# Moving the low half of one weight chunk behind each of five norms from VectorE to GpSimd

## What is computed

```python
x = x + 0.5 * rmsnorm(swiglu(rmsnorm(x, pre0), ffn_in0, ffn_out0), post0)
h = rmsnorm(x, pre1)                      # the next norm needs the whole new x
x = x + rmsnorm(mixer(h), post1)
x = x + 0.5 * rmsnorm(swiglu(rmsnorm(x, pre2), ffn_in1, ffn_out1), post2)
# between layer 0 and 1: kv = rmsnorm(x, kvin) @ w_dkv, shared keys and values
```

## Time and profile before

| what | value |
|---|---|
| runs | 1562.04 us median of 3 (1561.0 to 2078.39) |
| profiled execution | 1565.18 us, span 1563.5 us |
| TensorE busy | 1488.2 us (95%) |
| VectorE busy | 910.7 us (58%) |
| ScalarE busy | 748.3 us (48%) |
| GpSimd busy | 164.9 us (11%) |
| mean granted TensorE clock | 0.979 |
| chain that ended last | TensorE 84%, VectorE 10%, ScalarE 3%, issue 2%, DMA 1% |

### The profile page before, as it was taken

One profiled execution on the slowest core, in us unless ns is written; L12 is line 12 of the kernel. 1 busy time (PEld: TensorE's weight loads), 2 busy tenths in 40 slices (PEclk: granted clock), 3 DMA queues, 4 the chain that ended last, 5 costly groups with the idle time before them and its releaser, 6 DMA issues.

```text
span 1563.5 us, 29706 instructions
## 1 busy us (share of the span) xinstructions
PE 1488.2 (95%) x11112; PEld 1388.6 (89%) x11112; DVE 910.7 (58%) x1499; ACT 748.3 (48%) x1195; POOL 164.9 (11%) x239
## 2 busy tenths in 40 slices
PE   7999998999898999999979999998999999999997
PEld 7999997999676889999969999996866678999997
DVE  4655437979765586554385555337645546655524
ACT  4555425778533455553264555334334444655422
POOL 0111000000312001110001111001023400111100
PEclk9999999999899999999999999999989999999999
DMA  5444342433321234444423434344257732544341
GB/s 202 162 145 150 140 156 90 164 131 135 117 90 57 88 108 161 144 151 139 157 108 145 151 144 158 137 153 161 71 150 229 228 135 90 179 143 159 136 155 67
DMA packets 45011, 218.43 MB, mean 140 GB/s; under 512 B 6065, under 2 KB 18482, under 8 KB 22402
## 3 DMA queue, kind: packets, MB, share of 16 engines
q1 hardware_dynamic: 38738, 192.70, 34.9%
q0 software_dynamic: 6192, 24.64, 4.8%
HBM read 210.55 MB, written 6.77 MB: 139 GB/s over the span
## 4 chain that ended last, share of the span: by engine, by line
PE 84%; DVE 10%; ACT 3%; issue 2%; DMA 1%; DVEq 0%; POOL 0%; SPq 0%; ACTq 0%
PE psum L240 15%; PE psum L241 15%; PE psum L245 14%; PE psum L292 7%; PE psum L294 7%; PE psum L293 7%; PE psum L2037 2%; PE psum L2076 2%; DVE w_lo L228 1%; ACT w_hi L221 1%; DVE x L359 1%; DVE y L355 1%; DVE h_lo L401 1%; PE psum L2063 1%; PE psum L1913 1%
## 5 line engine op out<-in xcount | busy, mean ns | idle before, releaser
L228 DVE TENSOR_TENSOR w_lo<-raw,w_hi 128x2048 fp32r<-128x2048 f32 x166 | 384.9, 2318 | 319.1 <-ACT w_hi L221 318.9
L221 ACT ACTIVATE w_hi<-raw 128x2048 fp32r<-128x2048 f32 x161 | 308.6, 1916 | 367.1 <-PE psum L294 221.9
L240 PE MATMUL psum<-h_hi,w_hi 128*128 128x320 f32 x1552 | 462.8, 312 | 6.7 <-issue 4.7
L241 PE MATMUL psum<-h_lo,w_hi 128*128 128x320 f32 x1552 | 460.4, 309 | 0.0
L240 PEld LDWEIGHTS psum<-h_hi,w_hi 128*128 128x128 f32 x1552 | 293.4, 189 | 8.5 <-issue 5.4
L241 PEld LDWEIGHTS psum<-h_lo,w_hi 128*128 128x128 f32 x1552 | 293.4, 189 | 0.5
L245 PE MATMUL psum<-h_hi,w_lo 128*128 128x320 f32 x1552 | 259.8, 309 | 0.0
L245 PEld LDWEIGHTS psum<-h_hi,w_lo 128*128 128x128 f32 x1552 | 236.0, 188 | 0.4 <-DVE w_lo L228 0.2
L292 PE MATMUL psum<-hid_hi,w_hi 128*128 (+1 forms) x704 | 217.6, 309 | 4.1 <-DVE f_g L535 4.1
L294 PE MATMUL psum<-hid_hi,w_lo 128*128 (+1 forms) x704 | 217.3, 309 | 0.0
L293 PE MATMUL psum<-hid_lo,w_hi 128*128 (+1 forms) x704 | 217.3, 309 | 0.0
(11 more groups left out here) (380 smaller groups left out, 1967.9 us busy)
## 6 DMA issues: line engine op xcount, KB each, us to landing
raw<-wts SPq DMA_DIRECT2D x166, 1024.0 KB, 4.8
h_plain<-cache_t POOLq DMA_DIRECT2D x44, 160.0 KB, 3.4
h_plain<-cache_t SPq DMA_DIRECT2D x44, 160.0 KB, 3.2
arena<-s POOLq DMA_DIRECT2D x4, 1024.0 KB, 6.5
sgs<-arena POOLq DMA_DIRECT2D x4, 1024.0 KB, 4.1
marena<-cache_t POOLq DMA_DIRECT2D x20, 160.0 KB, 3.3
marena<-cache_t SPq DMA_DIRECT2D x20, 160.0 KB, 3.0
raw<-cache_c SPq DMA_DIRECT2D x16, 128.0 KB, 3.2
```

Source lines behind the costliest of these rows:

```text
L221: act.activation(w_hi[c0 % 2][:, :], raw[c0 % 2][:, :], ACT.Copy).then_inc(hi_ready, 1)
L228: eng.tensor_tensor(w_lo[c0 % 2][:, :], raw[c0 % 2][:, :], w_hi[c0 % 2][:, :].bitcast(F32), ALU.subtract).then_inc(lo_ready, 1)
L240: pe.matmul(outs[n], wtile(w_hi, c0, n * K + k), src_hi(k), start=(k == 0), stop=False)
L241: pe.matmul(outs[n], wtile(w_hi, c0, n * K + k), src_lo(k), start=False, stop=False)
```

## The change

residual_dve loses its last step and the argument for it. GpSimd gets five calls of split_lo, for the same five chunks, each ahead of the work that stood next in its queue. split_lo is the same function: it waits for `w_hi` of the chunk and for `w_lo` of the chunk before, makes one 128x2048 subtraction, and raises lo_ready. At the first boundary the call stands ahead of the issue of the `hist` transfer.

```diff
-        def residual_dve(dve, s, pre=None, q=0, c1=None):
+        def residual_dve(dve, s, pre=None, q=0):
...
             low(KT - 1)
             square_sum(KT - 1)
-            if c1 is not None:
-                split_lo(dve, c1)
...
             ffn_pool(pool, 0)
+            split_lo(pool, BASE["gates"] + 1)
             pool.wait_ge(chunk_done, BASE["gates"])
             pool.dma_start(arena[:, A_HIST:A_HIST + 24 * DEC_B * 3], io["hist"]).then_inc(s0_landed, 16)
             gdn_in_pool(pool)
             for g in range(NG):
                 core_pool(pool, g)
+            split_lo(pool, BASE["ffn1"] + 1)
             ffn_pool(pool, 1)
+            split_lo(pool, BASE["kv"] + 1)
             kv_pool(pool)
             ffn_pool(pool, 2)
+            split_lo(pool, BASE["dq"] + 1)
             pool.wait_ge(con_landed, 32)
             pool.wait_ge(chunk_done, BASE["dq"] + 2)
...
+            split_lo(pool, BASE["ffn3"] + 1)
             ffn_pool(pool, 3)
...
-            residual_dve(dve, 0, pre=(1, gpre(1)), q=1, c1=BASE["gates"] + 1)
+            residual_dve(dve, 0, pre=(1, gpre(1)), q=1)
...
```

More of the change, by code:

```diff
@@ L2489, in _ @@
             post_dve_sum(dve, 1, full(1), c1=BASE["ffn1"] + 1)
-            residual_dve(dve, 1, pre=(2, gpre(2)), q=2, c1=BASE["ffn1"] + 1)
+            residual_dve(dve, 1, pre=(2, gpre(2)), q=2)
             dve.wait_ge(rpre_ready, 3)
@@ L2496, in _ @@
             post_dve_sum(dve, 2, half(2), c1=BASE["kv"] + 1)
-            residual_dve(dve, 2, pre=(3, gkv), q=3, c1=BASE["kv"] + 1)
+            residual_dve(dve, 2, pre=(3, gkv), q=3)
             kv_dve(dve)
@@ L2500, in _ @@
             post_dve_sum(dve, 3, half(3), c1=BASE["dq"] + 1)
-            residual_dve(dve, 3, pre=(5, gpre(4)), q=4, c1=BASE["dq"] + 1)
+            residual_dve(dve, 3, pre=(5, gpre(4)), q=4)
             mla_q_dve(dve)
@@ L2506, in _ @@
             post_dve_sum(dve, 4, full(4), c1=BASE["ffn3"] + 1)
-            residual_dve(dve, 4, pre=(6, gpre(5)), q=5, c1=BASE["ffn3"] + 1)
+            residual_dve(dve, 4, pre=(6, gpre(5)), q=5)
             dve.wait_ge(rpre_ready, 6)
```

## The result

The changed kernel takes 1581.11 us in the median of 4 runs (1575.27 to 1584.87), against 1563.08 us in the median of 4 for the kernel before on the same chip: 1.0117 times as long, 95% interval 1.0075 to 1.0158. One of the four runs before took 2078.39 us and is left out of the ratio; without it their median is 1562.04 us. That is 18.0 us more by the medians and 18.2 us by the ratio; the forecast was 19.5 us more, 1581.5 us.

A forecast was written before the change was run, and what follows sets the result against it. VectorE's residual sets the pace at the five norm boundaries; elsewhere TensorE, busy 95%, does. Boundary costs net of returns, 15.0 us, plus 4.5 us of clock gave 19.5 us more, median 1581.5 us; forecast 1575 to 1587, range 1568 to 1590.

The forecast's parts named there:

- GpSimd's time: At each of five norm boundaries, GpSimd's 128x2048 subtraction was taken as 4.7 us, with ends 4.4 and 5.7.
- two lines through the small rows: Estimates of GpSimd's subtraction from 128 and 256 columns, 4.36 us, and from 128 and 320 columns, 4.76 us.
- Its start: At the ffn1 boundary, GpSimd starts 0.1 us after VectorE's cast, about 0.9 us before the first residual instruction.
- The hold: At each boundary, VectorE's first residual instruction is held until 0.15 us before GpSimd's end, delaying the residual 3.6 us.
- d: Delay of VectorE's whole residual at each boundary: 3.6 us, 3.3 to 4.6 with the ends, zero if nothing is shared.
- one overlap of 0.64 us: VectorE's `w_lo`, begun inside a GpSimd product, took 2.78 us where 2.28 is usual, an extension of 0.50.
- nothing shared: Rival: VectorE's residual keeps its pace beside GpSimd, returns stand alone, about 3 us, 1559 us; chance 6%.
- shared evenly: Rival: GpSimd lets VectorE through in turns, delay near 2 us a boundary, 7 us in all, 1569 us; chance 8%.
- The returns: Behind the boundaries, 2.0 us come back at gates and 1.0 at dq; ffn1, kv and ffn3 count 0.
- The clock: TensorE's longer hole before its first high product brings half clock: 1.5 us each at ffn1, dq and ffn3, 4.5 us.
- two holes of about the same length: TensorE holes of 4.70 and 3.95 us in the trace that came with a granted clock of 0.50.
- `hist`: Its transfer issues behind GpSimd's subtraction, about 5 us later; first use is 13 us later and more, so no cost.

The follow-up runs named there:

- the second measurement: The changed kernel itself, unaltered, measured again on the same chip: 1580.42 us, ratio 1.0105.
- x1: Against the kernel before, VectorE's subtraction stays and GpSimd makes the same low half first at the five places: 1584.03 us, ratio 1.0135.
- x8: Against the kernel before, VectorE's own subtraction moved from behind the residual to right behind the cast, GpSimd unused: 1563.38 us, ratio 1.0015.
- x6: Against the changed kernel, GpSimd's subtraction runs behind the residual instead of ahead of it: 1580.68 us, ratio 1.0129.
- x5: Against the kernel before, GpSimd makes 1024 of the 2048 columns, VectorE the rest behind the residual: 1571.04 us, ratio 1.0055.
- x11: Against x10, 40 instead of 20 filler matmuls at the kernel's start: 1563.08 us, ratio 0.9998 to the kernel before.
- x10: Against the kernel before, more filler matmuls in TensorE's two longest holes, at kv and dq: 1559.76 us, ratio 0.9985.

## Why the prediction was right, step by step

- *GpSimd's time.* 4.50 us against 4.7 taken, in the bounds of 4.4 and 5.7. Of the two lines through the small rows one had too low and one too high a slope (0.00203 and 0.00224 us a column); from 1024 columns (2.345 us) to 2048 it is 0.0021. (The figure of the Trainium skill, "GPSIMD Engine Reference", section "Performance versus the Vector engine", 4497 ns, agrees with the trace's median of 4502 ns.)
- *Its start.* 0.1 us behind the cast. Right.
- *The hold.* d was 3.39 us, taken 3.6; the whole difference is GpSimd's time. Five times 3.39 is 17.0 us against 18. Both assumptions under it, that the first one keeps the other off entirely and that VectorE gets in some 0.15 us before GpSimd's end, hold from 1.9 to 4.5 us of GpSimd time, though they were read out of one overlap of 0.64 us. The rivals "nothing shared" and "shared evenly" fall with the 3.88 us of L355.
- *The returns.* gates 2.10 (2.0 taken), dq 1.06 (1.0), ffn1 0.09, kv 0.03 and ffn3 0.16 (0). This was the step with most reasoning in it, and it held because each return was traced to the next thing that is late: at kv ScalarE's `w_hi`, at ffn1 the `w_hi` behind `r_pre`. TensorE's 4.4 us of waits at L281, the visible prize, returned 3.4 us, of which 3.2 came at gates and dq, where the transfers start sooner. x1 and x8 show them twice more.
- *The clock.* 4.5 us taken, at the three boundaries named; 3.2 and 4.7 us in two profiles, and 3.8 us by medians when the hole is filled. Single boundaries were 0.9 to 1.9 us, where 1.5 was taken for each. At gates and kv the clock fell too and cost nothing, as argued from their slack. That it would fall was read from two holes of about the same length; that it can also fall behind holes of 1.9 and 2.3 us, and need not, the prediction didn't see.
- *`hist`.* Free in the kernel after, as said, though its issue came 6.8 us later than before (252.52 and 259.30) and not 5. It was free only by the 13 us between issue and first use, and x6 used these up.
- The account's 16.8 to 18.3 us stand below the 19.5 because the hold is smaller by 1.0 us in all, the returns are larger by 0.4 us, and the clock came to between 1.3 us less and 0.2 us more.
- *Luck.* The mechanism was right term by term, but that the median of 1581.11 us lies within 0.4 us of the forecast is chance: the four runs spread over 9.6 us, and the second measurement was 1580.42 us.
- Of the expectations behind it, that of x6 failed, since neither the queue behind a late GpSimd nor the clock behind a longer wait at L281 was priced; that of x5 was low by 4 to 5 us, of which 1.0 is clock at ffn1 and the rest unexplained; that of x11 wasn't borne out.

## What to carry to other kernels

Before moving elementwise work to an idle GpSimd, look at what VectorE does in the same microseconds: if it is an operation on two SBUF tensors on the critical path and GpSimd will read SBUF, count GpSimd's time less its head start as added to the path; here it was, whole, though GpSimd was idle 89% of the time. What fitted VectorE's idle time cost nothing that could be measured, and a write without a read did not hold VectorE; the full 2048 columns were cheaper on VectorE itself, in the same place (1.19 against 3.39 us a boundary). And a freed engine's wait is worth what the next late thing leaves of it: follow it one step further before counting it.

## What of the hardware was not expected

- A GpSimd copy that reads one tensor holds VectorE's two-operand operation off as the subtraction does (1.26 us instead of 0.49), while a memset of the same size lets it through (0.49). I had weighed only two against two operands.
- Where TensorE's clock falls in the long parts changes between executions of one kernel enough to hide a third of this effect: mean granted clocks of 0.979 and 0.972 in two profiles of the kernel after, spans of 1573.2 and 1579.3 us. With levels of 1.00 and 0.50 these means stand for 66 and 88 us at the lower one.
- Whether filled holes add up is not shown: x10 gained 2.4 us (0.9972 to 0.9997), and x11, with more filled, nothing that can be measured (0.998 to 1.0016).
